# Triangular inverse of the recurrence heads in two groups of four, the two largest levels without masks

## The chip, the cores and the metric

The kernel runs on one core of one Trainium2 chip. The metric is device time in microseconds (us). TensorE's clock has two levels, 1.2 and 2.4 GHz; the profile gives the granted clock as a share of the higher one.

## What is computed

One decoder layer on 1024 tokens of width 1024, in float32: a SwiGLU block, a token mixer, cross attention over 256 memory tokens, a second SwiGLU block and a last norm. The change lies in the token mixer, which runs two recurrences side by side: RWKV-7 with 8 heads of 64 and mLSTM with 4 heads of 128.

```python
def step(state, xs):                       # RWKV-7, one token
    r_t, w_t, k_t, v_t, kk_t, b_t = xs
    sa = jnp.einsum('bhvk,bhk->bhv', state, -kk_t)
    state = (state * w_t[:, :, None, :] + sa[..., None] * b_t[:, :, None, :]
             + v_t[..., None] * k_t[:, :, None, :])
    return state, jnp.einsum('bhvk,bhk->bhv', state, r_t)
```

A chunk of 128 tokens is done at once. For each of the 8 heads that asks for the inverse of a 128 x 128 unit lower triangular matrix, I + A. The mLSTM is computed in chunks of 128 tokens too (num, den, the state C and n, then a norm over each head).

## The kernel before, in words

Large products (lines 540 to 561, each weight tile split in a high and a low part) make up most of the time. Between them stands the mixer loop (`iteration`, one function for each engine: GpSimd from line 452, TensorE from 653, ScalarE from 1114, VectorE from 1455). It makes one pass for each of 8 chunks (NSEG); a pass also finishes the output of the chunk before, and starts the next one's small products (`ahead`). The order of the work is written out by hand: each engine issues its instructions in the order of its function, and waits for the steps of others by name (`F` for the recurrence, `M` for the mLSTM, `B` for the output of the chunk before, `l_` for ahead).

The inverse is built by doubling. U starts as I minus the transposed first subdiagonal blocks (am0; A0 on TensorE, line 769, U0 on VectorE, line 1544). Each level n = 1 to 6 joins blocks of size 2^n:

- GpSimd masks A to the blocks of the level, AL (line 491, 1024 elements a partition, two buffers).
- TensorE makes W from AL and U (line 777, eight heads in one go), and V, the transpose of U, by products with the identity (line 785).
- ScalarE copies W to Wr (line 1171) and V to Tr (line 1174).
- TensorE makes E = Tr, Wr (line 810), and VectorE subtracts it from U (line 1558).

At level n the Tr used is the transpose of U of level n - 1; for level 1 GpSimd makes it (T0, line 485). Then one Newton step follows: F = A, U (line 832), Q on VectorE (1578) with I - U from GpSimd (IU, line 501), UQ (line 840), Uf (1580). Then TensorE issues ahead(i + 1), for which ScalarE makes `lora` (lines 1100 and 1101, signal "ad"), and then Wst (845), Z (849), the gate (853). The next pass begins with U (703, 704) and Y (716 to 718) of this chunk.

Between the levels stand the mLSTM's products (num 827, den 789, dC 798, dN 819, mean 803, var 806), and fillers, `stay_awake(bank, n)`, n products of 128 x 512 with the identity whose result nobody reads. All engines work on one PSUM bank pair for each of g0 (E), g1 (W), g2 (V); m0 and m1 are the mLSTM's.

In the mLSTM the reciprocal of the denominator (line 1554) stands on VectorE ahead of the update of level 4; mean stands on TensorE in level 5, var in level 6, and ScalarE takes the root of the variance with Ln and Exp (lines 1179, 1181), loads the table of Tanh (1183), and then copies Tr (1185) and does ahead (1187). VectorE's functions `gram`, copy_predicated through a mask, take A, Mu, B and Mv out of PSUM.

## Time and profile before

| what | value |
|---|---|
| median of 3 runs | 3461.13 us (3453.54 to 3461.25) |
| span of the profiled execution | 3460.0 us |
| time of the profiled execution around the span | not given |
| TensorE matmuls busy | 3232.1 us, 93% |
| TensorE weight loads busy | 2658.4 us, 77% |
| VectorE busy | 1126.6 us, 33% |
| ScalarE busy | 616.8 us, 18% |
| GpSimd busy | 1323.6 us, 38% |

Busy times of different engines overlap. A matmul's row gives its time from start to modelled end, so matmuls that follow one another overlap by part of it, and their pace is read from their starts. A released wait is written as [idle before <- what released it].

### The profile page before, as it was taken

What the parts mean: (1) busy time and instruction counts of PE and PEld (TensorE: products, weight loads), DVE (VectorE), ACT (ScalarE), POOL (GpSimd) and SP (SyncE); (2) the same over time, 40 slices, a digit from 0 to 9 for tenths busy, and PEclk for the clock granted to TensorE, in tenths of its full rate; (3) what the DMA queues carried; (4) which work ended last, traced back from release to release, by engine and by line L of the source; (5) the groups of instructions that cost most, each with busy time, mean ns of one, the idle gap of its engine ahead of it and who ended that gap; (6) DMA issues with size and microseconds to landing.
All of it is one profiled execution on the core that took longest, in us unless ns stands there. A gap on an engine that the chain in (4) does not pass through costs nothing.

```text
span 3460.0 us, 40298 instructions
## 1 busy us (share of the span) xinstructions
PE 3232.1 (93%) x15718; PEld 2658.4 (77%) x15718; DVE 1126.6 (33%) x918; ACT 616.8 (18%) x840; POOL 1323.6 (38%) x658
## 2 busy tenths in 40 slices
PE   5999999989999997999999996889979799999997
PEld 4888888867888886777777775679878588888885
DVE  4111111145450204554554544553033411111114
ACT  2100000011021212333333321111140210000001
POOL 2333333333433433443343433347303233333332
PEclk9999999999999997888888887997999899999998
DMA  2111111121222221011100104312101011111111
GB/s 109 49 49 49 48 49 48 45 96 69 95 98 101 89 84 46 27 29 29 29 25 22 29 7 155 140 49 79 49 6 41 32 49 49 49 49 49 49 43 67
DMA packets 85589, 196.42 MB, mean 57 GB/s; under 512 B 5648, under 2 KB 44688, under 8 KB 84504
## 3 DMA queue, kind: packets, MB, share of 16 engines
q1 hardware_dynamic: 68464, 136.86, 12.2%
q10 hardware_dynamic: 17064, 58.70, 4.4%
q8 instruction: 45, 0.74, 0.1%
q14 instruction: 16, 0.13, 0.0%
HBM read 158.80 MB, written 36.70 MB: 57 GB/s over the span
## 4 chain that ended last, share of the span: by engine, by line
PE 74%; issue 11%; POOL 5%; DVE 5%; ACT 2%; DMA 1%; DVEq 0%; ACTq 0%; POOLq 0%; PEldq 0%
PE G L543 22%; PE G L544 22%; PE G L545 22%; PE G L674 1%; POOL AL L491 1%; PE G L919 1%; PE G L606 1%; DMA ysg<-y_d 1%; DVE nt L1353 1%; POOL Tr L485 1%; PE G L898 1%; DVE nh L1378 0%; PE G L900 0%; POOL wlo L520 0%; PE G L899 0%
## 5 line engine op out<-in xcount | busy, mean ns | idle before, releaser
L543 PE MATMUL G<-hhi,whi 128*128 128x512 f32 x2544 | 998.2, 392 | 59.4 <-DVE hlo L1382 44.7
L517 POOL TENSOR_TENSOR whi<-raw,cst 128x1024 fp32r<-128x1024 f32 (+1 forms) x231 | 437.9, 1896 | 1587.1 <-PE G L545 1540.5
L544 PE MATMUL G<-hlo,whi 128*128 128x512 f32 x2544 | 996.4, 392 | 0.0
L545 PE MATMUL G<-hhi,wlo 128*128 128x512 f32 x2544 | 996.2, 392 | 0.0
L543 PEld LDWEIGHTS G<-hhi,whi 128*128 128x128 f32 x2544 | 481.9, 189 | 169.0 <-issue 48.2
L520 POOL TENSOR_TENSOR wlo<-raw,whi 128x1024 fp32r<-128x1024 f32 (+1 forms) x231 | 569.5, 2466 | 18.1
L545 PEld LDWEIGHTS G<-hhi,wlo 128*128 128x128 f32 x2544 | 481.4, 189 | 100.8
L544 PEld LDWEIGHTS G<-hlo,whi 128*128 128x128 f32 x2544 | 481.5, 189 | 100.1
L1411 DVE TENSOR_TENSOR s<-s,G 128x1024 f32<-128x1024 f32 x44 | 53.7, 1221 | 727.4 <-PE G L545 727.4
L543 PE MATMUL G<-ahi,whi 128*128 128x512 f32 x704 | 273.9, 389 | 0.0
L544 PE MATMUL G<-alo,whi 128*128 128x512 f32 x704 | 273.9, 389 | 0.0
L545 PE MATMUL G<-ahi,wlo 128*128 128x512 f32 x704 | 273.9, 389 | 0.0
L1397 DVE SCALAR_TENSOR_TENSOR xT<-G,xT 128x1024 f32 (+1 forms) x64 | 78.3, 1224 | 422.7 <-PE G L545 422.7
L1025 ACT ACTIVATE s<-G 128x1024 f32<-128x1024 f32 x44 | 45.3, 1029 | 651.8 <-PE G L545 651.7
L545 PEld LDWEIGHTS G<-ahi,wlo 128*128 128x128 f32 x704 | 132.1, 188 | 27.5
L544 PEld LDWEIGHTS G<-alo,whi 128*128 128x128 f32 x704 | 132.1, 188 | 27.4
L543 PEld LDWEIGHTS G<-ahi,whi 128*128 128x128 f32 x704 | 132.1, 188 | 27.4
L1413 DVE TENSOR_TENSOR alo<-s,ahi 128x1024 f32 x44 | 124.7, 2833 | 59.6 <-ACT ahi L1027 59.6
L1027 ACT ACTIVATE ahi<-s 128x1024 f32 x44 | 46.7, 1061 | 483.6 <-DVE s L1411 483.6
L491 POOL TENSOR_TENSOR AL<-Am,cst 128x1024 fp32r<-128x1024 f32 x48 | 120.3, 2529 | 1.1 <-PE G L674 1.1
L689 PE MATMUL G<-idr 128*128 128x512 f32 x384 | 112.2, 423 | 0.0
L1558 DVE TENSOR_TENSOR Ur<-Ur,G 128x1024 fp32r<-128x1024 f32 x48 | 58.5, 1219 | 125.6 <-PE G L674 125.6
(312 smaller groups left out, 3699.9 us busy)
## 6 DMA issues: line engine op xcount, KB each, us to landing
raw<-in_wg SPq DMA_DIRECT2D x44, 512.0 KB, 3.4
raw<-in_wu SPq DMA_DIRECT2D x44, 512.0 KB, 3.4
raw<-in_wd SPq DMA_DIRECT2D x32, 512.0 KB, 3.4
raw<-in_ml_in SPq DMA_DIRECT2D x16, 512.0 KB, 3.5
zml_d<-po ACTq DMA_DIRECT2D x16, 512.0 KB, 2.7
gates_d<-po ACTq DMA_DIRECT2D x16, 512.0 KB, 2.7
zm<-zml_d SPq DMA_DIRECT2D x8, 1024.0 KB, 5.6
...
```

What stands on the lines that cost most here:

```text
L491: tt(AL[:, n % 2], Am[:], copies(C_LEV + n * P), ALU.mult).then_inc(*F.sig(f"am{n}"))
L517: nc.gpsimd.tensor_tensor(whi[:, k, 0:w], raw[:, k, 0:w], cst[:, C_ZERO:C_ZERO + 1].to_broadcast([P, w]), ALU.add).then_inc(hi_made, 1)
L520: nc.gpsimd.tensor_tensor(wlo[:, k, 0:w], raw[:, k, 0:w], whi[:, k, 0:w].bitcast(F32), ALU.subtract).then_inc(split_made, 1)
L543: nc.tensor.matmul(dst, wh, hi, start=start, stop=False)
L544: nc.tensor.matmul(dst, wh, lo, start=False, stop=False)
L545: return nc.tensor.matmul(dst, wl, hi, start=False, stop=stop)
L689: nc.tensor.matmul(bank, idr[:, 0:P], idr[:], start=True, stop=True)
L1027: activation(ahi[:, i * 2 + r, :], s1[:], ACT.Copy).then_inc(a_hi, 1)
L1397: stt(x_, flat(bank_dve(c.dve + r)[:]), scale, x_, ALU.mult, ALU.add).then_inc(dve_free, 1)
L1411: tt(s1[:], s0[:], flat(bank_dve(c.dve + r)[:]), ALU.mult).then_inc(dve_free, 1)
L1413: tt(alo[:, i * 2 + r, :], s1[:], ahi[:, i * 2 + r, :].bitcast(F32), ALU.subtract).then_inc(a_lo, 1)
L1558: tt(flat(Ur[:]), flat(Ur[:]).bitcast(F32), flat(g0[:]), ALU.subtract).then_inc(*F.sig(f"U{n}"))
```

## The change

The eight heads are divided into set a (heads 0 to 3) and set b (4 to 7). Each step of the inverse is issued for a and then for b: the masks, U0, W, V, the copies, E and the update. W and V of a set give one signal (WV), and V at level n is the transpose that E of the same level uses, so T0 goes and level 1 has a V. Levels 5 and 6 use Ar, a copy of the whole of A, in place of a mask; their update writes only the blocks that the level adds. Am begins as the identity, so that F holds (I + A) U and Q needs no IU. Mv's product moves ahead of B's. Of the mLSTM, num, den, dC and dN stand behind E of levels 2 to 5, the reciprocal behind the updates of level 3, mean behind V of the Newton step, and var behind UQ. ScalarE copies Tr of the Newton step ahead of Ln, Exp and the table. The fillers around levels 1 to 6 go; before UQ there are 4 in place of 8. On GpSimd the output's three steps stand behind all masks.

```diff
+SETS = ("a", "b")
+MASKED = 4
...
-            pool.wait_ge(*f_dve.at("am0", i))
-            tt(Tr[:], copies(C_ID), AL[:, 0].bitcast(F32), ALU.subtract).then_inc(*F.sig("T0"))
-            for n in range(1, LEVELS):
-                if n == 2:
-                    pool.wait_ge(*F.at("T0", i))
-                if n >= 2:
-                    pool.wait_ge(*f_pe.at("am0T" if n == 2 else f"W{n - 2}", i))
-                tt(AL[:, n % 2], Am[:], copies(C_LEV + n * P), ALU.mult).then_inc(*F.sig(f"am{n}"))
...
+            for n in range(1, MASKED + 1):
+                for e, x in enumerate(SETS):
+                    if n == 1:
+                        pool.wait_ge(*f_dve.at(f"A{x}", i))
+                    else:
+                        pool.wait_ge(*f_pe.at(f"A0{x}" if n == 2 else f"WV{n - 2}{x}", i))
+                    part = slice(e * RC, (e + 1) * RC)
+                    tt(AL[:, n % 2, part, :], Am[:, part, :], copies(C_LEV + n * P, RC),
+                       ALU.mult).then_inc(*F.sig(f"am{n}{x}"))
+            pool.wait_ge(*m_pe.at("den", i))
+            tt(CN[:], CN[:], Eb[:, :, SEG - 1:SEG].unsqueeze(1).to_broadcast([P, 2, MH, SEG]),
+               ALU.mult).then_inc(*M.sig("dec"))
+            if back:
+                output()
             pool.wait_ge(*m_dve.at("yc", i))
             tt(mysq[:], hm[:], hm[:], ALU.mult).then_inc(*M.sig("ysq"))
-            pool.wait_ge(*f_dve.at(f"U{LEVELS - 1}", i))
-            tt(Uf[:], copies(C_ID), Ur[:].bitcast(F32), ALU.subtract).then_inc(*F.sig("IU"))
...
+            def four(dst, e, left, right):
+
+                for n in range(e * RC, (e + 1) * RC):
+                    last = nc.tensor.matmul(dst[:, e, n % RC * P:(n % RC + 1) * P], left[:, n, :], right(n),
+                                            start=True, stop=True)
+                return last
+
             stay_awake(g2[:, 0, :], 3)
-            pe.wait_ge(*f_dve.at("am0", i))
-            for n in range(NH):
-                last = nc.tensor.matmul(flat(g1[:])[:, n * P:(n + 1) * P], AL[:, 0, n, :], idr[:, 0:P], start=True, stop=True)
-            last.then_inc(*F.sig("am0T"))
-            stay_awake(g2[:, 0, :], 3)
+            for e, x in enumerate(SETS):
+                pe.wait_ge(*f_dve.at(f"am0{x}", i))
+                pe.wait_ge(*f_dve.at(f"A{x}", i))
+                four(g1, e, AL[:, 0], lambda n: idr[:, 0:P]).then_inc(*F.sig(f"A0{x}"))
+            pe.wait_ge(*b_dve.at("ve", j))
+            gram(kap, rho, g2).then_inc(*F.sig("Mv"))
             pe.wait_ge(*f_dve.at("Mu", i))
             gram(kap, alpha, g0).then_inc(*F.sig("B"))
             for n in range(1, LEVELS):
-                pe.wait_ge(*f_dve.at(f"U{n - 1}", i))
-                pe.wait_ge(*f_pool.at(f"am{n}", i))
-                eight(g1, AL[:, n % 2], Ur).then_inc(*F.sig(f"W{n}"))
-                if n == 1:
-                    stay_awake(g2[:, 0, :], 4)
-                    pe.wait_ge(*f_pool.at("T0", i))
-                    pe.wait_ge(*f_dve.at("B", i))
-                else:
-                    pe.wait_ge(*(f_dve.at("Mv", i) if n == 2 else f_act.at(f"Tc{n - 2}", i)))
-                    for h in range(NH):
-                        last = nc.tensor.matmul(flat(g2[:])[:, h * P:(h + 1) * P], Ur[:, h, :], idr[:, 0:P], start=True,
-                                                stop=True)
-                    last.then_inc(*F.sig(f"V{n - 1}"))
+                for e, x in enumerate(SETS):
+                    pe.wait_ge(*f_dve.at(f"U{n - 1}{x}", i))
+                    if n <= MASKED:
+                        pe.wait_ge(*f_pool.at(f"am{n}{x}", i))
+                    elif n == MASKED + 1:
+                        pe.wait_ge(*f_act.at(f"Ar{x}", i))
+                    four(g1, e, AL[:, n % 2] if n <= MASKED else Ar, lambda n: Ur[:, n, :])
+                    if n == 1:
+                        pe.wait_ge(*f_dve.at("Mv", i))
+                    four(g2, e, Ur, lambda n: idr[:, 0:P]).then_inc(*F.sig(f"WV{n}{x}"))
+                for e, x in enumerate(SETS):
+                    if n == 1:
+                        pe.wait_ge(*f_dve.at("B", i))
+                    pe.wait_ge(*f_act.at(f"Tc{n}{x}", i))
+                    four(g0, e, Tr, lambda n: Wr[:, n, :]).then_inc(*F.sig(f"E{n}{x}"))
+                if n == 2:
+                    pe.wait_ge(*m_act.at("vtok", i))
+                    pe.wait_ge(*m_dve.at("qe", i))
+                    for h in range(MH):
+                        dst = m1[:, h * SEG:(h + 1) * SEG]
+                        nc.tensor.matmul(dst, mvtok[:, h, :], Pb[:, h, :], start=True, stop=False)
+                        last = nc.tensor.matmul(dst, CN[:, 0, h, :], qe[:, h, :], start=False, stop=True)
+                    last.then_inc(*M.sig("num"))
...
                 if n == 5:
-                    pe.wait_ge(*m_dve.at("C", i))
-                    nc.tensor.matmul(m0, con(C_ONES), flat(hm[:]), start=True, stop=True).then_inc(*M.sig("mean"))
-                if n == 6:
-                    pe.wait_ge(*m_pool.at("ysq", i))
...
-                if n == 2:
-                    stay_awake(g0[:, 0, :], 4)
-                pe.wait_ge(*f_act.at(f"Wc{n}" if n == 1 else f"Tc{n - 1}", i))
-                eight(g0, Tr, Wr).then_inc(*F.sig(f"E{n}"))
...
-                elif n > 2:
-                    stay_awake(g1[:, 0, :], 5)
...
                     pe.wait_ge(*m_dve.at("hm", i))
                     for h in range(MH):
                         last = nc.tensor.matmul(m1[:, h * SEG:(h + 1) * SEG], kw[:, h, :], con(C_ONES),
                                                 start=True, stop=True)
                     last.then_inc(*M.sig("dN"))
...
-            pe.wait_ge(*f_dve.at(f"U{LEVELS - 1}", i))
+
+            for x in SETS:
+                pe.wait_ge(*f_dve.at(f"U{LEVELS - 1}{x}", i))
             eight(g1, Am, Ur[:].bitcast(F32)).then_inc(*F.sig("F"))
-            pe.wait_ge(*f_act.at(f"Tc{LEVELS - 2}", i))
             for n in range(NH):
                 last = nc.tensor.matmul(flat(g2[:])[:, n * P:(n + 1) * P], Ur[:, n, :], idr[:, 0:P], start=True, stop=True)
-            last.then_inc(*F.sig(f"V{LEVELS - 1}"))
-            stay_awake(g0[:, 0, :], 8)
-            pe.wait_ge(*f_act.at(f"Tc{LEVELS - 1}", i))
+            last.then_inc(*F.sig("V"))
+            pe.wait_ge(*m_dve.at("C", i))
+            nc.tensor.matmul(m0, con(C_ONES), flat(hm[:]), start=True, stop=True).then_inc(*M.sig("mean"))
+            stay_awake(g0[:, 0, :], 4)
+            pe.wait_ge(*f_act.at("Tc", i))
             pe.wait_ge(*f_dve.at("Q", i))
             eight(g0, Tr, Qr).then_inc(*F.sig("UQ"))
+            pe.wait_ge(*m_pool.at("ysq", i))
+            nc.tensor.matmul(m1, con(C_ONES), flat(mysq[:]), start=True, stop=True).then_inc(*M.sig("var"))
             if more:
...
+
             if not front:
+                output_root()
                 store_output(j)
...
+            def half(ap, e):
+                return ap[:, e * RC:(e + 1) * RC, :].rearrange("p n t -> p (n t)")
+
+            for e, x in enumerate(SETS):
+                act.wait_ge(*f_dve.at(f"A{x}", i))
+                activation(half(Ar, e), half(Am, e), ACT.Copy).then_inc(*F.sig(f"Ar{x}"))
+            if back:
+                output_root()
             for n in range(1, LEVELS):
-                act.wait_ge(*f_pe.at(f"W{n}", i))
-                activation(flat(Wr[:]), flat(g1[:]), ACT.Copy).then_inc(*F.sig(f"Wc{n}"))
-                if n > 1:
-                    act.wait_ge(*f_pe.at(f"V{n - 1}", i))
-                    activation(flat(Tr[:]), flat(g2[:]), ACT.Copy).then_inc(*F.sig(f"Tc{n - 1}"))
+                for e, x in enumerate(SETS):
+                    act.wait_ge(*f_pe.at(f"WV{n}{x}", i))
+                    activation(half(Wr, e), g1[:, e, :], ACT.Copy).then_inc(*F.sig(f"Wc{n}{x}"))
+                    activation(half(Tr, e), g2[:, e, :], ACT.Copy).then_inc(*F.sig(f"Tc{n}{x}"))
                 if n == 3:
                     act.wait_ge(*m_pe.at("den", i))
                     activation(flat(aden[:]), m0, ACT.Abs).then_inc(*M.sig("aden"))
+            act.wait_ge(*f_pe.at("V", i))
+            activation(flat(Tr[:]), flat(g2[:]), ACT.Copy).then_inc(*F.sig("Tc"))
             act.wait_ge(*m_dve.at("ve", i))
             activation(flat(mrs[:]), flat(mve[:]), ACT.Ln).then_inc(*M.sig("lnv"))
             act.wait_ge(*M.at("lnv", i))
             activation(flat(mrs[:]), flat(mrs[:]), ACT.Exp, scale=-0.5).then_inc(*M.sig("rsv"))
...
             if more:
                 nc.scalar.preload_act_table(ACT.Tanh)
-            act.wait_ge(*f_pe.at(f"V{LEVELS - 1}", i))
-            activation(flat(Tr[:]), flat(g2[:]), ACT.Copy).then_inc(*F.sig(f"Tc{LEVELS - 1}"))
             if more:
                 ahead(i + 1, gate=False)
...
-            gram("A", Am, g1, C_LOW)
-            dve.wait_ge(*F.at("A", i))
-            tt(AL[:, 0], Am[:], copies(C_LEV), ALU.mult).then_inc(*F.sig("am0"))
...
+            def first(e):
+
+                dve.wait_ge(*f_pe.at(f"A0{SETS[e]}", i))
+                tt(Ur[:, four(e), :], copies(C_ID, RC), three(g1[:, e, :]), ALU.subtract).then_inc(*F.sig(f"U0{SETS[e]}"))
+
+            def update(n, e):
+
+                done = F.sig(f"U{n}{SETS[e]}")
+                dve.wait_ge(*f_pe.at(f"E{n}{SETS[e]}", i))
+                if n <= MASKED:
+                    tt(Ur[:, four(e), :], Ur[:, four(e), :].bitcast(F32), three(g0[:, e, :]), ALU.subtract).then_inc(*done)
+                    return
+                b = 1 << n
+                for top in range(0, P, 2 * b):
+                    block = ts(Ur[top:top + b, four(e), top + b:top + 2 * b], three(g0[top:top + b, e, :])[:, :, top + b:top + 2 * b],
+                               -1.0, None, ALU.mult)
+                block.then_inc(*done)
+
+            for e, x in enumerate(SETS):
+                tt(AL[:, 0, four(e), :], three(g1[:, e, :]), copies(C_LEV, RC), ALU.mult).then_inc(*F.sig(f"am0{x}"))
+                nc.vector.copy_predicated(Am[:, four(e), :], copies(C_LOW, RC).bitcast(U32),
+                                          three(g1[:, e, :])).then_inc(*F.sig(f"A{x}"))
...
             gram("Mu", Mu, g0, C_UPEQ)
...
+            first(0)
+            dve.wait_ge(*f_pe.at("Mv", i))
             stt(flat(qe[:]), zm[:, 0:MH, :].rearrange("p h t -> p (h t)"), ML_SCALE, flat(Eb[:]), ALU.mult,
                 ALU.mult).then_inc(*M.sig("qe"))
+            gram("Mv", Mv, g2, C_UPEQ)
+            first(1)
+            dve.wait_ge(*b_dve.at("S", j))
+            dve.wait_ge(*f_pe.at("B", i))
+            tt(S0s[:], St[:], Pi[:, :, 0:1].to_broadcast([P, RC, HD]), ALU.mult).then_inc(*F.sig("S0s"))
             gram("B", Bm, g0, C_UP)
             for n in range(1, LEVELS):
-                if n == 4:
+                update(n, 0)
+                update(n, 1)
+                if n == 2 and back:
+                    output_norm()
+                if n == 3:
                     dve.wait_ge(*m_act.at("aden", i))
                     tt(aden[:], aden[:], nmb[:], ALU.max).then_inc(*M.sig("dmax"))
                     dve.wait_ge(*M.at("dmax", i))
                     nc.vector.reciprocal(flat(aden[:]), flat(aden[:])).then_inc(*M.sig("rec"))
+                if n == 4:
                     dve.wait_ge(*M.at("rec", i))
                     tt(flat(hm[:]), m1, flat(aden[:]), ALU.mult).then_inc(*M.sig("hm"))
-                dve.wait_ge(*f_pe.at(f"E{n}", i))
-                tt(flat(Ur[:]), flat(Ur[:]).bitcast(F32), flat(g0[:]), ALU.subtract).then_inc(*F.sig(f"U{n}"))
-                if n == 1:
-                    dve.wait_ge(*b_dve.at("S", j))
-                    dve.wait_ge(*f_pe.at("Mv", i))
...
-                if n == 4:
+                if n == 5:
...
-                if n == 5:
-                    dve.wait_ge(*m_pe.at("mean", i))
-                    stt(flat(hm[:]), m0, -1.0 / P, flat(hm[:]), ALU.mult, ALU.add).then_inc(*M.sig("yc"))
+            dve.wait_ge(*f_pe.at("F", i))
+            tt(Qr[:], copies(C_ID), three(flat(g1[:])), ALU.subtract).then_inc(*F.sig("Q"))
+            dve.wait_ge(*m_pe.at("mean", i))
+            stt(flat(hm[:]), m0, -1.0 / P, flat(hm[:]), ALU.mult, ALU.add).then_inc(*M.sig("yc"))
+            dve.wait_ge(*f_pe.at("UQ", i))
+            tt(flat(Uf[:]), flat(Ur[:]).bitcast(F32), flat(g0[:]), ALU.add).then_inc(*F.sig("Uf"))
             dve.wait_ge(*m_pe.at("var", i))
             ts(flat(mve[:]), m1, 1.0 / P, ML_EPS, ALU.mult, ALU.add).then_inc(*M.sig("ve"))
-            dve.wait_ge(*f_pool.at("IU", i))
-            dve.wait_ge(*f_pe.at("F", i))
-            tt(flat(Qr[:]), flat(Uf[:]), flat(g1[:]), ALU.subtract).then_inc(*F.sig("Q"))
-            dve.wait_ge(*f_pe.at("UQ", i))
-            tt(flat(Uf[:]), flat(Ur[:]).bitcast(F32), flat(g0[:]), ALU.add).then_inc(*F.sig("Uf"))
...
-        for m in (Am, Bm, Mv, Mu, St, dec, CN):
+        step(nc.vector.tensor_copy(Am[:], con(C_ID).unsqueeze(1).to_broadcast([P, NH, P])))
+        for m in (Bm, Mv, Mu, St, dec, CN):
```

## Rows read from the trace of the kernel before

**Rows 1.** the page's first line.

```profile
span 3460.0 us, 40298 instructions
```

**Rows 2.** the first subtraction of each pass (line 1544), instructions that write Ur: op, count, min/median/max ns, first and last start.

```profile
L1544 DVE TENSOR_TENSOR Ur<-cst,G x8: 1199/1202/1210, 1344.7 to 2000.7; 128x1024 fp32r<-128x1024 f32 x8
```

**Rows 3.** U0 to Wst, Wst to U0, twice: length, busy PE PEld DVE ACT POOL, granted clock.

```profile
1721.00:1765.35 44.35, 41.54 (x301) 34.88 (x299) 24.51 (x25) 15.68 (x19) 25.97 (x15) 1.00 0.07 21
1765.35:1812.90 47.55, 47.54 (x270) 36.65 (x270) 23.59 (x32) 16.39 (x36) 13.60 (x10) 0.71 0.12 33
1812.90:1862.74 49.84, 46.15 (x301) 39.00 (x299) 26.69 (x25) 15.79 (x19) 25.99 (x15) 0.90 0.07 18
1862.74:1908.90 46.16, 46.15 (x270) 35.61 (x270) 23.60 (x32) 16.40 (x36) 13.61 (x10) 0.74 0.12 34
```

**Rows 4.** timeline of one pass, W of level 2, then all of level 5: start us, us, what.

```profile
1728.40 1.11 PE L674 MATMUL G<-Ur,AL 128*128 128x128 f32 x8
...
1747.24 1.09 PE L674 MATMUL G<-Ur,AL 128*128 128x128 f32 x8
...
1748.17 1.06 PE L785 MATMUL G<-idr,Ur 128*128 128x128 f32 x8
1748.37 1.03 ACT L1171 ACTIVATE Wr<-G 128x1024 fp32r<-128x1024 f32 x1 [4.15 <-PE G L674]
...
1749.29 1.02 ACT L1174 ACTIVATE Tr<-G 128x1024 fp32r<-128x1024 f32 x1
...
1750.36 1.11 PE L674 MATMUL G<-Wr,Tr 128*128 128x128 f32 x8 [0.22 <-ACT Tr L1174]
...
1751.51 1.22 DVE L1558 TENSOR_TENSOR Ur<-Ur,G 128x1024 fp32r<-128x1024 f32 x1 [2.76 <-PE G L674]
...
1752.86 0.32 PE L674 MATMUL G<-Ur,AL 128*128 128x128 f32 x1 [0.18 <-DVE Ur L1558]
```

**Rows 5.** groups by line over one pass, U0 to U0: count, busy us, mean ns.

```profile
L689 PEld LDWEIGHTS G<-idr 128*128 128x128 f32 x48 | 8.3, 189 | 1.2
```

**Rows 6.** timeline, operations of 512 elements from PSUM on VectorE and ScalarE.

```profile
1718.57 0.68 DVE L1472 TENSOR_SCALAR yve<-G 128x512 f32<-128x512 f32 x1
...
1804.03 0.60 ACT L1151 ACTIVATE atok<-G 128x512 f32<-128x512 f32 x1 [3.30 <-PE G L662]
```

**Rows 7.** timeline of level 3 and 4: the first product of den, the reciprocal.

```profile
1736.94 1.07 PE L789 MATMUL G<-Pb,cst 128*128 128x512 f32 x2
...
1741.64 3.35 DVE L1554 RECIPROCAL aden<-aden 128x512 f32<-128x512 f32 x1
```

**Rows 8.** timeline of TensorE behind the levels: F, UQ, Wst, U.

```profile
1758.41 2.05 PE L674 MATMUL G<-Ur,Am 128*128 128x128 f32 x16
...
1763.03 1.00 PE L674 MATMUL G<-Qr,Tr 128*128 128x128 f32 x8
...
1765.35 1.58 PE L845 MATMUL G<-Uf,atok 128*64 128x128 f32 x16 [0.22 <-DVE Uf L1580]
...
1773.96 0.43 PE L703 MATMUL G<-Zm,Uf 128*128 128x64 f32 x2
```

**Rows 9.** timeline of GpSimd and ScalarE behind the levels.

```profile
1753.41 1.04 POOL L499 TENSOR_TENSOR Pb<-hm 128x512 f32<-128x512 f32 x1 [7.23 <-DVE hm L1573]
...
1760.30 1.28 ACT L1183 ACT_TABLE_LOAD   x1
...
1762.84 0.31 ACT L1101 ACTIVATE lora<-zs 64x128 f32<-64x128 f32 x1
```

**Rows 10.** the pass before: TensorE's wait at level 4, the clock after it, two groups at it.

```profile
1653.18 1.16 PE L819 MATMUL G<-cst,kw 128*128 128x128 f32 x8 [1.35 <-DVE hm L1556]
...
1656.00:1658.00 2.00, 2.00 (x8) 1.64 (x8) 0.00 (x0) 1.32 (x2) 0.00 (x0) 0.50 0.00 0
...
1655.49 1.91 PE L785 MATMUL G<-idr,Ur 128*128 128x128 f32 x8
1657.20 2.02 PE L803 MATMUL G<-hm,cst 128*128 128x512 f32 x2
```

52 lines of the change are left out of this document (14 added, 38 removed).

## Prediction, made before the change was run

> **What bounds the kernel now.** I read the page first, then the granted clock and busy shares by stretch, then the engines' timeline of one pass of the mixer loop, then the waits. The profiled execution spans 3460.0 us [rows 1], 1.1 us under the median of 3461.13 us; the page gives no time for what lies around the span, so I make the sum as a difference and set it on the median. The change touches only the mixer loop: eight passes over 128 tokens each. Its first subtraction from the identity, once a pass, starts at 1344.7 us in the first pass and at 2000.7 us in the last, so a pass takes 656.0/7 = 93.7 us [rows 2].
>
> A pass has two halves [rows 3]. From U0 (the start of the inverse) to Wst (its first use) an undisturbed pass takes 44.35 us at full clock (2.4 GHz); the next one takes 49.84 us with a granted clock of 0.90, which is about 10 us at the lower level, 1.2 GHz. From Wst to the next U0 it takes 47.55 or 46.16 us, at 0.71 and 0.74, with TensorE busy throughout. So the first half is a chain of handovers and the second is TensorE's own time.
>
> In the chain one level reads as follows [rows 4]: W on TensorE from 1747.24, two copies by ScalarE (Wr 1748.37, Tr 1749.29), E from 1750.36, the update by VectorE from 1751.51, the next W at 1752.86. That is 5.62 us, and no engine is full. Between the links stand filler matmuls (stay_awake): 48 in a pass [rows 5].
>
> **The head, to level 2.** VectorE now copies and masks A in halves and does Mv's copy ahead of the second half of U0, and TensorE does A0 in halves. By halves of the durations [rows 4, 6], U0a comes at 1721.0 as U0 does now, V1a waits for Mv's copy (about 1724.7), E1a for B's copy (about 1726.8), and W2a can start at about 1728.3, against 1728.40 now [rows 4]. The head brings nothing. GpSimd's T0 and IU and its masks of levels 5 and 6 go; the queue of masks runs ahead of TensorE from level 3 on, so leaving two of them out gives nothing either. The two copies into Ar add about 1.2 us on an idle ScalarE. The identity copied into Am once costs nothing that is seen.
>
> **The levels.** For four heads: W and V are eight matmuls, 1.11 us; the two copies are half of 0.92 us plus one of 0.60 us, 1.06 us [rows 4, 6]; E of four, 0.64 us; an update of 512 elements 0.68 us [rows 6]; about 0.3 us of handovers. Level: 3.8 us, and the other group fits under it, since both take 24 matmuls at 0.116 us (0.93/8, from W at 1747.24 to V at 1748.17 [rows 4]), 2.8 us of TensorE. The last two updates write blocks of 128 to 256 elements; I have no row of that form on PSUM and take them as 0.2 to 0.68 us, which moves the sum by under 1 us. In TensorE's fixed order the mLSTM products now stand behind E of both groups and ahead of the next W: den is 1.07 us for its two wide matmuls and about 0.7 for the eight behind them [rows 7], num about 1.75 us (16 at 0.11), dN 0.9 us (8). At level 4 the reciprocal of 3.35 us [rows 7] starts after den and holds U4a: 1.85 us more. Five levels 19.0 + 1.75 + 1.75 + 1.85 + 0.9, and 0.7 for the second group at the end, give 26.0 us from W2 to F; now it is 1758.41 - 1728.40 = 30.0 us [rows 4, 8]. **Term 1: -4.1 us a pass**, at full clock.
>
> **Behind the levels.** F to UQ stays at 4.6 us: without GpSimd's IU, Q comes sooner, but V, mean, four fillers and Tr stand in its place. Then the order turns against the change. Now mean and var of the mLSTM are done within levels 5 and 6, and ScalarE has finished Ln, Exp and the table load by 1761.6, ahead of UQ [rows 8, 9]. After the change mean stands behind V and var behind UQ. TensorE's ahead(i+1) needs lora from ScalarE, which issues it only behind Ln and Exp (which wait for var) and the table load; and Wst stands behind ahead(i+1). From the start of UQ: UQ 1.15, var 1.05, ve 0.7, Ln and Exp 1.35, table load 1.3, the two lora activations 0.65, the lora matmuls 1.05 = 7.25 us [rows 6, 8, 9]. Now it is 1765.35 - 1763.03 = 2.32 us [rows 8]. **Term 2: +4.9 us a pass** in the seven that have a successor. GpSimd's square (1.04 us [rows 9]) fits under UQ. Queued behind this wait are Wst, Z and the gate on TensorE, and W1m, Zm and gout on ScalarE.
>
> **The clock in the levels.** 35 of the 48 fillers go. At five to a level they are a third of what TensorE does there. In the disturbed pass TensorE waited 1.35 us for hm at level 4, and two stretches of 2 us later its clock stood at 0.50 [rows 10]; eight matmuls then took 1.91 us instead of 1.06. That happened with the fillers in place. With less work in the levels I expect falls in every pass. At 1.2 GHz the 24 matmuls take 24 x 0.213 (1.71/8, from V at 1655.49 to the next at 1657.20) = 5.1 us a level, and num, den, dC and dN double. All of it at the lower clock would be 14.6 us more from W1 to F; none of it is zero. I take half clock for half of the stretch, whose loss per us is about 0.33 us: **term 3: +5 us**, bounds 0 and 14.6. A level at the lower clock is still shorter than one now, which is why it isn't more.
>
> **The clock behind the levels.** In term 2 TensorE idles from the end of var to the lora matmuls, about 4.1 us, three times the wait that preceded the fall above. So Wst, Z and the gate, which now run at full clock, start at the lower one. Wst to U is 1773.96 - 1765.35 = 8.6 us now, all TensorE [rows 8]. Bounds: 0 and 8.6 us; with Wst, Z and the gate (4.2 us) doubled and part of the fillers I take 5.0, less 1.4 because the second half was shorter by that where the clock had fallen before it (47.55 and 46.16 [rows 3]). **Term 4: +3.6 us.** The Trainium skill ("TensorE: Matmul & The Clock Gate", section "What's actually happening") says that the throttled clock is the default and that activity releases it. By that rule the pause alone costs clock whatever the fillers did; with the trace's fall after 1.35 us of waiting it agrees. Without rule and row the sum would be terms 1 and 2 alone.
>
> **Sum.** 91.9 us for an undisturbed pass (44.35 + 47.55) - 4.1 + 4.9 + 5 + 3.6 = 101.3 us, 7.6 us above the mean of 93.7. Seven times that is 53 us; the eighth pass has no ahead, so terms 1 and 3 cancel there: about 0. Median 3461 + 53 = 3514 us.
>
> **Rivals.** What a measurement of this kernel can tell from no change is about 0.3%, or 10 us.
> A, faster: the clock holds. The two groups follow each other so closely that TensorE is busier than I think, and four fillers with mean bridge the end. Then a pass is 92.7 us at most, 1.0 below the mean: -7 us, and -5 in the last pass: 3449 us. If ScalarE's chain also hid under other work, 4.9 us a pass more would go, to some 3415 us. It decides where terms 3 and 4 together stay under 1 us a pass. Against it: 4.1 us without a matmul. Chance 0.13.
> B: the clock holds in the levels and falls only behind them: terms 1, 2 and 4 give 96.3 us a pass, +18 and -4: 3475 us. For it: undisturbed passes have none. Chance 0.19.
> C: the lower clock all through the levels: 14.6 in place of 5, 110.9 us a pass, 17.2 above the mean, and 10 in the last: about 3590 us. Against it: num, den and F are dense. 0.08.
> D: the change doesn't act: the groups don't overlap because ScalarE or VectorE, each doing four or two half-size operations a level, becomes the bound. Four copies are 2.0 us and two updates 1.3 us of 3.8, so no. It would take term 1 away, 4.1 us in each of eight passes: 3547 us. Chance 0.05.
> The forecast has 0.55.
>
> **Numbers.** Range 3460 to 3550 us: it takes in B, the forecast with terms 3 and 4 between 1 and 13 us, and D; it leaves out A and C. Faster is A, 0.13. Same (3451 to 3471 us) is a third of B and the low end of the forecast, 0.06 + 0.03 = 0.09. Slower is the rest: 0.13 of B, 0.52 of the forecast, C and D, 0.78.
>
> **What would show it.** W of level 2 should start about 7.3 us after U0a; W2 to F 26 us where the clock is 1.00; the wait of the lora matmuls for ScalarE about 4 us a pass, new in the waits; UQ to Wst 7 us instead of 2.3; the granted clock between U0 and Wst under 0.9 in every pass, and 0.5 at Wst; U0 to U0 about 101 us. I am wrong if the clock at Wst is 1.00, if U0 to F stays at full clock, or if var's root is taken before UQ.

## The result and the profile after

The changed kernel takes 3571.36 us (median of 4 runs, 3549.63 to 3575.88) against 3461.19 us for the kernel before: ratio 1.0314, 95% interval 1.0284 to 1.0345. It is slower, as forecast, but 57 us above the forecast of 3514 us and 21 us above the range. One of the four executions, the one of 3549.63 us, had a higher mean granted clock, 0.901 against 0.896 and 0.897 in the others.

The page's first lines and clock row of the changed kernel (line numbers from here on are those of the changed kernel and of the experiments, not of the listing above):

```profile
span 3569.8 us, 40207 instructions
PE 3290.9 (92%) x15502; PEld 2735.0 (77%) x15502; DVE 1112.5 (31%) x1006; ACT 642.6 (18%) x960; POOL 1242.3 (35%) x658
PEclk9999999989999987767676777996899899999998
```

and the clock row of the kernel before:

```profile
PEclk9999999999999997888888887997999899999998
```

The span is 109.8 us longer [rows 1], and TensorE's busy time grew by 58.8 us (3290.9 - 3232.1) with fewer instructions (40207 against 40298): the same products took longer, and the rest is waiting. The clock rows say where: over the mixer loop, from the sixteenth digit on, most digits are 6 or 7, where before most are 8.

One pass of the loop, cut at U0, F, UQ, Wst, U and at U0 of the next pass (length, busy time of PE, PEld, DVE, ACT, POOL, granted clock, DMA share and GB/s):

```profile
1557.16:1601.56 44.40, 38.62 (x218) 35.40 (x216) 21.98 (x29) 13.41 (x25) 12.76 (x10) 0.69 0.07 21
1601.56:1607.49 5.93, 5.93 (x31) 5.28 (x32) 1.91 (x2) 1.02 (x1) 0.00 (x0) 0.76 0.00 0
1607.49:1615.82 8.33, 4.14 (x28) 2.95 (x26) 4.68 (x6) 3.16 (x5) 4.12 (x4) 0.73 0.00 0
1615.82:1625.49 9.67, 9.67 (x67) 8.36 (x65) 3.94 (x6) 5.75 (x14) 2.46 (x3) 0.88 0.58 163
1625.49:1663.00 37.51, 37.50 (x208) 28.17 (x208) 15.40 (x26) 12.12 (x24) 10.43 (x9) 0.68 0.00 0
```

Before, the same cuts of an undisturbed pass are 37.4, 4.6, 2.32, 8.6 and 38.9 us ([rows 3, 8] hold them: 44.35 = 37.4 + 4.6 + 2.3). All seven full passes after are alike, 105.8 us (the first 106.1); before, four take 91.9 us and three 96.0 to 96.4, mean 93.7 [rows 2, 3]. Every part grew but the last, which is 1.4 us shorter.

Inside the first stretch the clock by level (head to V1; V1 and level 1; level 2 and num; level 3 and den; level 4 with the reciprocal; level 5; level 6 and dN):

```profile
1557.16:1561.00 3.84, 3.23 (x37) 2.97 (x36) 3.19 (x5) 0.00 (x0) 1.80 (x2) 1.00 0.55 160
1561.00:1564.61 3.61, 3.12 (x20) 2.70 (x20) 2.53 (x4) 2.17 (x4) 2.52 (x2) 0.84 0.30 84
1564.61:1573.69 9.08, 8.76 (x41) 8.57 (x42) 4.40 (x7) 2.17 (x4) 2.54 (x2) 0.50 0.00 0
1573.69:1580.82 7.13, 6.53 (x36) 5.21 (x36) 1.71 (x3) 2.06 (x4) 0.00 (x0) 0.76 0.00 0
1580.82:1587.67 6.85, 4.25 (x35) 3.78 (x34) 5.90 (x4) 2.66 (x5) 5.89 (x4) 0.98 0.00 0
1587.67:1595.10 7.43, 7.11 (x32) 6.92 (x33) 2.20 (x6) 2.17 (x4) 0.00 (x0) 0.50 0.00 0
1595.10:1601.56 6.46, 5.63 (x27) 5.25 (x26) 2.05 (x3) 2.17 (x4) 0.00 (x0) 0.50 0.00 0
```

and TensorE's timeline at the two places where it fell:

```profile
1559.50 0.66 PE L769 MATMUL G<-Ur,AL 128*128 128x128 f32 x4
1560.78 0.66 PE L769 MATMUL G<-idr,Ur 128*128 128x128 f32 x4 [0.61 <-DVE Mv L1476]
...
1562.98 1.84 PE L769 MATMUL G<-Wr,Tr 128*128 128x128 f32 x8 [0.46 <-DVE Bm L1476]
1564.61 1.05 PE L769 MATMUL G<-Ur,AL 128*128 128x128 f32 x4
```

W1 of set a starts 2.3 us and W2 7.45 us behind U0 (forecast 7.3). Between them TensorE pauses twice, 0.61 us for Mv and 0.46 us for B, in place of fillers; four products of level 2 then take 1.05 us instead of 0.66. The second fall follows level 4, in which TensorE is busy for 4.25 of 6.85 us and at its end waits 2.00 us for U of that level, which VectorE updates behind the reciprocal:

```profile
1587.67 1.11 PE L769 MATMUL G<-Ur,Ar 128*128 128x128 f32 x4 [2.00 <-DVE Ur L1556]
```

The two falls are of about the same size. From the clocks of the seven rows (twice what is missing to 1.00, times the length), 13.7 us at the lower level lie in levels 1 to 3 and 14.2 us from level 4 to F.

The tail, ScalarE first, then TensorE:

```profile
1605.85 1.02 ACT L1187 ACTIVATE Tr<-G 128x1024 fp32r<-128x1024 f32 x1 [5.97 <-PE G L830]
1610.51 0.63 ACT L1189 ACTIVATE nmb<-qe 128x512 f32<-128x512 f32 x1 [3.64 <-DVE qe L1609]
1611.17 0.63 ACT L1191 ACTIVATE nmb<-nmb 128x512 f32<-128x512 f32 x1
1611.82 1.28 ACT L1193 ACT_TABLE_LOAD   x1
...
1613.45 0.31 ACT L1100 ACTIVATE lora<-zs 64x128 f32<-64x128 f32 x1
```

```profile
1607.49 1.00 PE L674 MATMUL G<-Qr,Tr 128*128 128x128 f32 x8
1608.62 1.12 PE L839 MATMUL G<-Pb,cst 128*128 128x512 f32 x2
1613.81 0.58 PE L647 MATMUL G<-lora,loraw 64*128 64x128 f32 x1 [4.06 <-ACT lora L1100]
...
1615.82 2.64 PE L844 MATMUL G<-Uf,atok 128*64 128x128 f32 x16
1618.39 2.00 PE L848 MATMUL G<-vtok,Bm 128*128 128x64 f32 x16
1620.23 1.11 PE L852 MATMUL G<-gsig,loraw 128*128 128x128 f32 x8
```

Read backwards, Wst waits for the lora products, these for lora, lora for the table, the table for Exp and Ln, and Ln for ve behind var behind UQ. That is the forecast chain; TensorE's pause is 4.06 us against 4.1 forecast. Wst takes 2.64 us instead of 1.58 [rows 8], but the gate at 1620.23 is at full clock again.

Not all of the 109.8 us is in the loop. The next phase starts 90.4 us later (2193.9 against 2103.5 us). Most of the rest is in the keys and values of the cross attention, in products that the change doesn't touch, from the first eviction of vx to the last: before, then after.

```profile
2360.30:2417.37 57.07, 56.18 (x336) 55.74 (x336) 28.96 (x13) 9.82 (x16) 37.65 (x15) 0.66 0.23 73
```

```profile
2455.12:2527.20 72.08, 71.82 (x337) 71.67 (x337) 24.29 (x13) 9.68 (x16) 36.15 (x15) 0.50 0.16 51
```

TensorE is busy throughout in both, yet after it sits at the lower clock from end to end: 15.0 us. In the profiled executions of the experiments below it ran at 0.50 twice more and at 0.66 or 0.67 seven times, and at 1.00 in the three that have fillers in it.

### The profile page after: what moved, and what is told of

It reads as the page before. It is cut to its first block, busy times and chain, and to the rows that moved or that the text cites. A ratio compares the mean times of both kernels' runs of the same rounds, so it can differ in the third digit from the quotient of the medians.

```text
span 3569.8 us, 40207 instructions
## 1 busy us (share of the span) xinstructions
PE 3290.9 (92%) x15502; PEld 2735.0 (77%) x15502; DVE 1112.5 (31%) x1006; ACT 642.6 (18%) x960; POOL 1242.3 (35%) x658
## 4 chain that ended last, share of the span: by engine, by line
PE 38%; issue 15%; POOL 5%; DVE 3%; ACT 2%; DMA 1%; POOLq 0%; DVEq 0%; ACTq 0%; PEldq 0%
PE G L543 10%; PE G L544 10%; PE G L545 10%; POOL AL L493 2%; PE G L769 1%; PE G L918 1%; PE G L899 1%; PE G L897 1%; PE G L898 1%; DMA ysg<-y_d 1%; DMA xT<-x_park 0%; ACT sx L1274 0%; PE G L606 0%; PE G L668 0%; POOL wlo L520 0%
## 5 line engine op out<-in xcount | busy, mean ns | idle before, releaser
L543 PEld LDWEIGHTS G<-hhi,whi 128*128 128x128 f32 x2544 | 482.0, 189 | 170.0 <-issue 47.8
L769 PE MATMUL G<-Wr,Tr 128*128 128x128 f32 x384 | 90.1, 376 | 21.5 <-ACT Tr L1182 17.3
L769 PEld LDWEIGHTS G<-Wr,Tr 128*128 128x128 f32 x384 | 76.0, 277 | 32.8 <-ACT Tr L1182 31.1
L1361 DVE TENSOR_TENSOR nt<-nt,nsq 128x1024 f32<-128x1024 f32 x40 | 82.1, 2052 | 50.0 <-ACT nsq L985 43.1
```

The lines of the kernel that those rows point to most:

```text
L543: nc.tensor.matmul(dst, wh, hi, start=start, stop=False)
L769: last = nc.tensor.matmul(dst[:, e, n % RC * P:(n % RC + 1) * P], left[:, n, :], right(n), start=True, stop=True)
L1361: tt(t, t, sq[:, n, :], ALU.add).then_inc(*nsq_dve.sig(f"add{n}"))
```

## The experiments

Three things could each have been the loss: the fillers, the place of the root, and the groups themselves. The first three kernels put back one, the other, and both; two more take the same two things out of the kernel before.

**Fillers back.** In the changed kernel, in levels 2 to 6:

```diff
+                if n > 1:
+                    stay_awake(g0[:, 0, :], 2)
                 for e, x in enumerate(SETS):
...
+                    elif e == 1:
+                        stay_awake(g0[:, 1, :], 1)
                     pe.wait_ge(*f_act.at(f"Tc{n}{x}", i))
...
                     last.then_inc(*M.sig("dC"))
+                    stay_awake(g1[:, 0, :], 5)
```

> The changed kernel with fillers put back where TensorE waits: two between WV and E and one between the two E in levels 2 to 6, five behind dC while VectorE takes the reciprocal. Nothing else. In the changed kernel U0 to F takes 44.4 us a pass at a granted clock of 0.69. Theory (the levels are short, and the lost fillers let the clock fall): U0 to F drops to 34 to 37 us with the clock at 0.9 or more, F to UQ to 4.6 to 5.0, UQ to Wst stays at 7 to 8.3; a pass of about 96 us in place of 105.8, some 75 us less in all, near 1.01 of the kernel before. Rival (the levels are long because the mLSTM's products and the two half-size handovers stand in TensorE's order; the clock only follows): 19 fillers lie in the way, U0 to F stays at 44 us or grows by up to 19 x 0.23 = 4 us.

Measured 3488.83 us, ratio 1.0099 (1.0065 to 1.0134). Passes take 97.3 to 98.9 us; U0 to F and UQ to Wst of one:

```profile
1639.30:1677.54 38.24, 35.70 (x238) 31.57 (x236) 22.03 (x29) 13.20 (x25) 12.86 (x10) 0.87 0.08 24
...
1682.11:1690.44 8.33, 4.13 (x27) 2.94 (x26) 4.69 (x7) 3.16 (x5) 4.07 (x4) 0.76 0.00 0
```

Twenty added products of 512 columns made the stretch 6.2 us shorter, and the tail, untouched, stays at 8.33 us. Of the 82.5 us that this kernel gains on the changed one, 14.5 are the vx stretch (57.6 us in the profiled execution here); nearly all of the rest is the loop.

**Root ahead of UQ.** Mean behind E of level 6, var in place of the four fillers, and VectorE's two steps with them:

```diff
-            stay_awake(g0[:, 0, :], 4)
+            pe.wait_ge(*m_pool.at("ysq", i))
+            nc.tensor.matmul(m1, con(C_ONES), flat(mysq[:]), start=True, stop=True).then_inc(*M.sig("var"))
             pe.wait_ge(*f_act.at("Tc", i))
             pe.wait_ge(*f_dve.at("Q", i))
             eight(g0, Tr, Qr).then_inc(*F.sig("UQ"))
-            pe.wait_ge(*m_pool.at("ysq", i))
-            nc.tensor.matmul(m1, con(C_ONES), flat(mysq[:]), start=True, stop=True).then_inc(*M.sig("var"))
```

> The changed kernel with mean behind E of level 6, var behind V and ahead of UQ (in place of the four fillers), and VectorE's yc and ve ahead of Q and Uf. Theory (var behind UQ makes ScalarE's root and table load late, and with them the lora matmuls): UQ to Wst drops from 8.3 us to 4.5 to 5.5, F to UQ stays within 1 us, a pass is 3 to 4 us shorter, 20 to 30 us in all. Rival (ScalarE's order alone decides, wherever var stands): UQ to Wst stays at 7.5 us or more. U0 to F stays at 44 us, give or take 1.5, by both.

Measured 3526.57 us, ratio 1.018 (1.0139 to 1.0222). UQ to Wst is 5.5 to 6.0 us. The gain, 44.8 us, is more than the 20 to 30 expected, for U0 to F moved too, to between 40.6 and 45.6 us, with no instruction of it changed but mean, where I had expected 44 give or take 1.5. Every pass still starts its levels at full clock and has the fall behind the head; what differs from pass to pass is the time at the lower clock after that, and why is open. The vx stretch is 72.1 us, as in the changed kernel.

**Both.**

> Both edits together. Theory: the gains add: U0 to F 34 to 37 us, UQ to Wst 4.5 to 5.5, a pass of 91 to 93 us, so within 0.5% of the kernel before. Rival (one clock fall is shared by both, so that mending one mends the other): no more than 2 us a pass better than the better of the two.

Measured 3467.82 us, ratio 1.0009 (0.9985 to 1.0033). So the two repairs take back 103.5 of the 110.2 us; alone they take 82.5 and 44.8. The vx stretch, which no edit touched, is in these numbers: 57.6 us with the fillers, 72.1 with the root ahead and 56.9 with both. Less what each gained there, the repairs took 68, 45 and together 88 us, so their gains add only in part. Passes take 93.6 to 95.0 us, above the 91 to 93 expected. One pass:

```profile
1627.70:1666.32 38.62, 36.52 (x239) 32.02 (x239) 22.02 (x29) 13.20 (x25) 12.82 (x10) 0.87 0.08 24
...
1670.30:1675.17 4.87, 2.16 (x24) 1.94 (x24) 4.07 (x6) 3.16 (x5) 0.18 (x1) 1.00 0.00 0
```

**The kernel before, without its 35 fillers.**

```diff
-            stay_awake(g2[:, 0, :], 3)
             pe.wait_ge(*f_dve.at("Mu", i))
...
-                    stay_awake(g2[:, 0, :], 4)
...
-                if n == 2:
-                    stay_awake(g0[:, 0, :], 4)
...
-                elif n > 2:
-                    stay_awake(g1[:, 0, :], 5)
...
-            stay_awake(g0[:, 0, :], 8)
+            stay_awake(g0[:, 0, :], 4)
```

> The kernel before with the same fillers taken out as in the change (35 of 48 a pass) and nothing else. Theory: the clock falls in the levels of every pass, U0 to F goes from a mean of 39.8 us to 43 to 48, a pass to 97 to 102 us in place of 93.7, 30 to 60 us slower in all. Rival (the fillers don't hold the clock; the copies and updates hide what TensorE loses): within 10 us of the kernel before, or faster, since 8 us of fillers a pass are gone.

Measured 3549.7 us, ratio 1.0256 (1.0219 to 1.0294). Every pass takes 102.4 us; U0 to F of one:

```profile
1653.50:1702.91 49.41, 41.73 (x214) 37.56 (x214) 23.73 (x22) 11.75 (x12) 21.51 (x12) 0.65 0.07 19
```

49.4 us at 0.65, where the groups take 44.4 at 0.69. Without the fillers the groups are worth about 5 us a pass. Not all of it is their shorter chain: they also spend less time at the lower level, 27.5 us against 34.6 (2 x 0.31 x 44.4 and 2 x 0.35 x 49.41).

**The kernel before, with the change's order of the root:** mean behind V, var behind UQ, Tr ahead of Ln and Exp, four fillers, IU ahead of the square.

```diff
+            pe.wait_ge(*m_dve.at("C", i))
+            nc.tensor.matmul(m0, con(C_ONES), flat(hm[:]), start=True, stop=True).then_inc(*M.sig("mean"))
+            stay_awake(g0[:, 0, :], 4)
             pe.wait_ge(*f_act.at(f"Tc{LEVELS - 1}", i))
...
             eight(g0, Tr, Qr).then_inc(*F.sig("UQ"))
+            pe.wait_ge(*m_pool.at("ysq", i))
+            nc.tensor.matmul(m1, con(C_ONES), flat(mysq[:]), start=True, stop=True).then_inc(*M.sig("var"))
```

> The kernel before (eight heads in one go, all its fillers in the levels) with only the order behind the levels as in the change: mean behind V, var behind UQ, four fillers in place of eight, VectorE's yc and ve and ScalarE's root where the change has them. Theory (that order costs its own time, whatever the levels do): UQ to Wst goes from 2.3 us to 7.3 to 8.5, F to UQ stays within 0.5 us, a pass is 5 to 7 us longer in seven of eight, 35 to 50 us in all, near 1.012 of the kernel before. Rival (the wait shows only because the levels end sooner in the change, and the time comes back in the half behind Wst, which is TensorE's own): under 15 us in all.

Measured 3527.15 us, ratio 1.0183 (1.0146 to 1.022). UQ to Wst, and Wst to U behind it:

```profile
1590.86:1599.19 8.33, 4.14 (x27) 2.94 (x25) 4.68 (x7) 3.16 (x5) 4.08 (x4) 0.85 0.00 0
1599.19:1613.01 13.82, 13.82 (x66) 11.94 (x64) 3.90 (x6) 5.75 (x14) 2.50 (x3) 0.60 0.41 114
```

The chain costs the same 8.33 us without groups. Behind it the clock stays low for most of Wst to U in every second pass (0.60, +5.2 us), and in the others costs 0.6 to 1.0 us. The 66 us in all are more than the 35 to 50 expected.

**Fillers in level 1 too.** The third kernel with seven more, into m0, which is free there:

```diff
                     if n == 1:
+                        if e == 0:
+                            stay_awake(m0, 3)
                         pe.wait_ge(*f_dve.at("Mv", i))
...
+                else:
+                    stay_awake(m0, 3)
...
+                        stay_awake(g0[:, 1, :] if n > 1 else m0, 1)
```

> The third experiment's kernel (fillers in the levels, root ahead of UQ) with fillers in level 1 too: three between W1a and V1a, three behind WV1b, one between the two E, into the mLSTM's free bank. The two stretches at the lower clock that were left between U0 and F begin in level 1. Theory (the clock alone keeps U0 to F at 38.4 us; the levels need 33 to 34 at full clock): the granted clock from U0 to F goes from 0.87 to 0.97 or more, U0 to F to 34 to 36 us, a pass to 91 to 93 us, 10 to 20 us less than the third, a ratio of 0.995 to 1.000. Rival (fillers add what the clock gives): U0 to F at 38 us or more.

Measured 3439.39 us, ratio 0.9943 (0.9924 to 0.9963). U0 to F:

```profile
1525.90:1560.38 34.48, 33.28 (x247) 28.24 (x246) 21.97 (x29) 13.10 (x25) 12.76 (x10) 1.00 0.10 27
```

Full clock in all eight passes. With the pauses for Mv and B filled, the first fall is gone, and 4.1 us with it; the whole is 28 us under the third kernel, more than the 10 to 20 expected. This is the kernel in which the groups' own worth can be read, both at full clock: 34.5 us against 37.4.

**The root out of the way.** ScalarE takes the mLSTM's Ln and Exp behind the next pass's load of the log and exp table, in place of ahead of Tanh's, and Tanh's table is loaded ahead of the copy Tr:

```diff
+            if back:
+                act.wait_ge(*m_dve.at("ve", j))
+                activation(flat(mrs[:]), flat(mve[:]), ACT.Ln).then_inc(*M.sig("lnv"))
+                act.wait_ge(*M.at("lnv", j))
+                activation(flat(mrs[:]), flat(mrs[:]), ACT.Exp, scale=-0.5).then_inc(*M.sig("rsv"))
```

> The kernel of e6_both_and_head with ScalarE's Ln and Exp of the mLSTM variance behind the table load that the next pass makes anyway, so that the table of Tanh is loaded and the lora activations are issued right behind the copy Tr. VectorE's Newton steps of the mLSTM then wait for it. Theory (what is left between UQ and Wst is ScalarE's root and table): UQ to Wst goes from about 5.1 us to 2.3 to 3, a pass 2 to 3 us shorter, 88.5 to 91 us, 0.985 to 0.993 of the kernel before: faster than both. Rival (the late root holds VectorE's part of the next pass and comes back ahead of A): U to A grows by 2 us or more and the pass stays.

Measured 3440.31 us (3423.29 to 3442.86), ratio 0.9914 (0.9884 to 0.9944). The two stretches, each at full clock:

```profile
1562.86:1565.28 2.42, 2.20 (x24) 1.94 (x24) 1.71 (x2) 0.55 (x3) 0.18 (x1) 1.00 0.00 0
1565.28:1573.89 8.61, 8.58 (x64) 7.30 (x64) 0.02 (x1) 6.50 (x16) 0.00 (x0) 1.00 0.10 30
```

A pass is 88.9 us in the mean, 2.3 less than in the kernel before it. The rival was right in part: from U to the next U0 the pass takes 39.3 to 39.8 us in place of 36.0 to 38.9, and TensorE now waits there for ScalarE's copy Un, 1.18 us in this pass. The time of the profiled execution hides the gain: its vx stretch took 72.1 us, against 57.5 there.

**Fillers in the keys and values.** The changed kernel with three products of 512 columns ahead of each group of that stretch:

```diff
+                                for _ in range(3):
+                                    nc.tensor.matmul(bank[:, m, :], whi[:, k, 0:P],
+                                                     memhi[:, 0:2, :].rearrange("p k t -> p (k t)"), start=True, stop=True)
                                 for t in range(KD):
```

> The changed kernel with three 512-column fillers ahead of each half unit in the second half of keys_values (the products for vx, far behind the mixer loop, untouched by the change) and nothing else. That stretch takes 57.4 us in the kernel before and 72.2 us in the changed one, where the clock stands at 0.50 all through. Theory (its products of 128 columns don't bring the clock back by themselves once it is low; the change only met it low): the clock is 0.9 or more, the stretch takes 45 to 58 us, the whole 12 to 25 us less than the changed kernel, near 1.025. Rival (something of the change, as the place of code or data, slows those products): the stretch stays at 70 us or more.

Measured 3543.41 us, ratio 1.0227 (1.0191 to 1.0263). The loop's passes stay at 105.8 us, and the stretch:

```profile
2450.20:2498.00 47.80, 47.54 (x380) 45.47 (x379) 26.10 (x13) 9.75 (x16) 38.07 (x15) 1.00 0.22 68
```

24.3 us less than in the changed kernel, with 42 of the 48 added products inside this cut.

**Masks at all levels:** the kernel with the root in the next pass, and MASKED = 6, so that GpSimd masks and W and the update are whole at levels 5 and 6.

```diff
-MASKED = 4
+MASKED = 6
```

> The kernel of e7_root_in_next_pass with masks and full updates at levels 5 and 6 too (MASKED = 6); the copies Ar are still made. Theory (GpSimd's masks run ahead of TensorE, so the two largest levels without masks bring next to nothing): U0 to F 34.5 us or up to 0.6 more for the two full-size updates (0.68 us in place of 0.58 and 0.42), a pass within 1 us of 88.9, whole within 8 us once the stretch of the key and value products is taken out. Rival (four more mask operations of 1.27 us hold GpSimd, and level 5 waits for them): U0 to F grows by 2 us or more.

Measured 3425.47 us, ratio 0.9902 (0.9888 to 0.9916). Most of the 15 us under the kernel without these masks is the vx stretch, 57.6 us in the profiled execution here against 72.1. But U0 to F is 33.4 us, 1.1 us less than without the masks. VectorE's maximum and GpSimd's decay of C and n, without the masks and then with them:

```profile
1543.69 1.88 DVE L1602 TENSOR_TENSOR aden<-aden,nmb 128x512 f32<-128x512 f32 x1 [1.75 <-ACT aden L1200]
1543.11 1.92 POOL L496 TENSOR_TENSOR CN<-CN,Eb 128x1024 f32<-128x1024 f32 x1 [7.59 <-PE G L817]
```

```profile
1543.02 0.69 DVE L1602 TENSOR_TENSOR aden<-aden,nmb 128x512 f32<-128x512 f32 x1 [1.75 <-ACT aden L1200]
1543.28 2.82 POOL L493 TENSOR_TENSOR AL<-Am,cst 128x512 fp32r<-128x512 f32 x2 [2.49 <-PE G L769]
1546.05 1.92 POOL L496 TENSOR_TENSOR CN<-CN,Eb 128x1024 f32<-128x1024 f32 x1
```

Without the masks GpSimd comes to the decay 0.6 us before VectorE comes to the maximum, which then lasts 1.88 us instead of 0.69: it ends 0.54 us behind the decay, as if it had waited for it. With them GpSimd is on a mask, started 0.26 us behind the maximum. The reciprocal, which stands behind the maximum, starts 1.2 us earlier in the pass. The Trainium skill ("SBUF — State Buffer", section "SBUF: two separate sides") says that a VectorE operation with two operands in SBUF and a GpSimd operation that reads SBUF lock a shared pair of ports for a whole instruction, first come first served. With these rows it agrees.

**The best parts together:** the root in the next pass, and the fillers in the keys and values.

> The kernel of e7_root_in_next_pass with the fillers of e8_fillers_in_keys_values. Theory: the two stretches are independent, the products for vx take 47.8 us in place of 72.1 in the profiled run of e7 (57.4 in the kernel before), a ratio of 0.984 to 0.988 of the kernel before, and the runs spread less. Rival (the clock won there is lost in the stretch behind it): 0.990 or more.

Measured 3414.13 us (3410.59 to 3415.48), ratio 0.9867 (0.9853 to 0.9881): faster than both kernels. Passes of 88.8 to 89.4 us, the vx stretch 47.7 us.

**Fillers in the second half.** 18 single fillers a pass among U, Y and dS, added to the kernel with the root in the next pass:

```diff
                     last = nc.tensor.matmul(dst, W1m[rows, r, :], S0s[rows, r, :], start=False, stop=True)
+                    if n < NH - 1:
+                        stay_awake(g0[:, 1, :], 1)
```

> The kernel of e7_root_in_next_pass with fillers in the half of a pass that runs at the lower clock: seven between the heads of U, seven between those of Y, four in dS, into a free half of a bank. U to A takes 32.7 us at a granted clock of 0.58. Theory (the clock falls there because products of 64 rows or columns count little, as in the levels): the clock rises to 0.8 or more and U to A drops to 26 to 30 us, though 18 fillers cost 4 us; a pass 84 to 87 us, 0.975 to 0.985 of the kernel before. Rival (these products keep the clock down whatever stands between them): U to A grows by 18 x 0.24 to 0.43 us, 4 to 8 us, a ratio of 1.00 or more.

Measured 3528.05 us, ratio 1.0196 (1.0182 to 1.0211). U to A, without these fillers and then with them:

```profile
1573.89:1606.82 32.93, 31.75 (x151) 23.17 (x150) 17.96 (x24) 7.68 (x16) 9.21 (x7) 0.59 0.14 40
```

```profile
1697.58:1743.36 45.78, 45.77 (x170) 29.07 (x169) 17.91 (x25) 7.81 (x16) 9.23 (x7) 0.55 0.10 29
```

My theory failed. The clock is 0.55, and the stretch grew by 0.7 us for each filler (12.9 us over 18), more than the rival's 4 to 8 us. The time at the lower level in it grew from 27 to 41 us (2 x 0.41 x 32.93 and 2 x 0.45 x 45.78). Here TensorE hardly waits, and the filler buys nothing.

**All of it, with the masks.**

> The kernel of e10 with GpSimd's masks, full copies into W and whole updates at levels 5 and 6 too, as in e9. My theory, from e9 beside e7: in the pass, GpSimd's two masks of level 6 stand ahead of its decay of C and n, so VectorE's maximum of the denominator no longer shares its time with that step (0.69 us for 1.88), and 8 passes are each some 0.4 to 1.1 us shorter. So this kernel is 3 to 9 us under e10's 3414.13 us: 3405 to 3411 us, ratio 0.984 to 0.986, U0 to F 33.4 us in place of 34.5. Rival: the gap between e7 and e9 came from the keys and values stretch alone (72.1 us in e7's profiled run, 57.6 in e9's); with the fillers in that stretch in both kernels it is 47.7 us here as in e10, and the two kernels are within 3 us of each other.

Measured 3415.29 us (3414.43 to 3416.23), ratio 0.9874 (0.9854 to 0.9894): as the rival had it, no gain over 3414.13, though not for its reason alone. The levels are about 1 us shorter in every pass (33.41 for 34.46 us in the third), but U to A takes 0.3 to 0.9 us longer in five of seven. The granted clock of that stretch is the same, 0.59 in the third pass of both; what is longer is TensorE's wait for ScalarE's copy Un, without the masks and then with them:

```profile
1586.34 0.69 PE L716 MATMUL G<-Mv,vtok 128*64 128x128 f32 x2 [1.28 <-ACT Un L1150]
```

```profile
1583.20 0.69 PE L716 MATMUL G<-Mv,vtok 128*64 128x128 f32 x2 [1.74 <-ACT Un L1150]
```

By the sixth pass it is 2.09 against 0.78 us. In the last pass it is the clock: Wst to U takes 8.85 us at 0.54 for 5.58 us at 1.00. So a part of what the levels won went into a wait further down, and a part was lost to the clock; at the last U0 3.5 us were left, and that stretch took 3.3 of them.

## Why the prediction was right in direction and wrong in size

Per pass, against an undisturbed one of 91.9 us:

| step | forecast | measured | from |
|---|---|---|---|
| term 1, levels at full clock | -4.1 | -2.9 | 34.5 for 37.4 us, fillers in all levels |
| term 3, clock in the levels | +5 | +9.9 | 44.4 for 34.5 us |
| F to UQ | 0 | +1.3 | 5.93 for 4.6 us, clock 0.76 |
| term 2, UQ to Wst | +4.9 | +6.0 | 8.33 for 2.32 us |
| term 4, Wst to U, and the second half | +5.0 - 1.4 | +1.1 - 1.4 | 9.67 for 8.62 us |
| sum | +9.4 | +13.9 | 105.8 for 91.9 us |

**The step that failed is term 3**, "half clock for half of the stretch": a granted clock of 0.69 over 44.4 us is 27.5 us at the lower level (2 x 0.31 x 44.4), not the 15 that 5 us at 0.33 stand for. The loss per us, 0.36 (9.9/27.5), was about right. I had placed the falls where I had seen one before, at the wait for hm. A fall came there, behind the wait for the update of level 4, and its 14.2 us are about what I took for the whole. The other, 13.7 us behind the head, I left out. The forecast itself has V1a waiting for Mv and E1a for B, some 1 us, and I counted these pauses in the critical path only and not in the clock. Behind them level 2 and part of level 3 run at 1.2 GHz. The runs separate the two: fillers in levels 2 to 6 take back 6.2 us (44.40 to 38.24), fillers in level 1 then 4.1 (38.62 to 34.48), and with both no stretch of the levels is at the lower clock.

The trace of before could have warned me. In the very pass that I read [rows 10], the clock also falls at the head, behind a wait for Mv, and the stretch of 2 us behind it is at 0.50:

```profile
1634.24 1.64 PE L785 MATMUL G<-idr,Ur 128*128 128x128 f32 x8 [0.69 <-DVE Mv L1468]
1636.00:1638.00 2.00, 2.00 (x7) 1.61 (x7) 0.90 (x2) 0.94 (x1) 0.98 (x1) 0.50 0.00 0
```

It could also have told me that a wait alone does not settle it: that wait for Mv, 0.69 to 0.76 us, stands in all eight passes, and the clock falls behind it in three; a wait of 1.35 to 1.44 us for hm stands in four, and the clock falls behind it in three.

The measured 9.9 us lies halfway between the 5 I took and case C, all of it, at 14.6, a figure for which the forecast shows no working. Seven passes with 4.9 us more than term 3 allowed are 34 of the 57 us by which the forecast was short.

**F to UQ** was costed at nothing because no work was added there; it inherited the low clock.

**Term 2** was right in mechanism to within 1.1 us: the pause of 4.06 us was forecast as 4.1. What I left out was that the products behind the pause start at the low clock: the lora products, from 1613.81 to Wst at 1615.82, take 2.0 us for the 1.05 of the sum. That it is the order and not the groups is shown from both sides: adding it to the kernel before gives the same 8.33 us, and with neither var nor the root in the way the stretch is 2.42. It is two moves: with mean and var ahead of UQ again the stretch is 4.87 us at full clock, 3.5 less, and ScalarE's root and table behind the copy Tr are the other 2.45 us.

**Term 4** was too large by 3.9 us. The clock fell, but came back by the gate. In the kernel before with the late root the full price (5.2 us) appears in every second pass, so the 5.0 was a real case, not this kernel's. That term 4 was too large hid most of what term 3 lacked: with it at its measured size the forecast would have been 3.9 us a pass lower, further from the result. That is luck.

**Term 1** was 1.2 us too large, and 1.1 of it has a cause that the runs show: the masks left out at levels 5 and 6 let GpSimd's decay meet VectorE's maximum. With them the stretch is 33.4 us, and the forecast was 33.3 (37.4 - 4.1). "Leaving two of them out gives nothing" was true, and the price of their absence was missed.

**Outside the passes.** The last pass, forecast at 0, gave +4.9 us: before, that pass took 39.4 us from U0 to F, after it took 44.4. The vx stretch gave +15.0 us, which no step of the forecast had. That makes 85.5 to the last U0, 90.4 to the end of the loop and 109.8 us in all; the 4.4 us between the loop and the vx stretch I did not trace.

Among the rivals, A fell with the first row of the clock. B fell too: the clock did not hold in the levels. C fell: 27.5 of 44.4 us were at the lower level, not all. D fell: the groups overlap, for 2.9 us at full clock and 5 without fillers. The idea behind the change is sound; with the waits refilled it is 0.6% under the kernel before (0.9943), and 0.9% with the root in the next pass (0.9914). The fillers in the keys and values make it 1.3%, but they have nothing to do with the groups, and the kernel before was not tried with them.

What stays open: why the vx stretch ran at 0.50 in three profiled executions and at 0.66 or 0.67 in eight, with the same instructions in it. The fillers show that it can be held at full clock, not what sets it off.
